# A norm factored out per token, a gather in halves, another load order, and attention by pairs of heads

## The reference

```
mod = silu(c) @ ada_w + ada_b                          # sh1, sc1, g1, sh2, sc2, g2
h = rmsnorm(x, norm_mix_g) * (1 + sc1) + sh1
x = x + g1 * conformer_conv(h)     # 1024 -> 2x1024, gate, 31 taps, layernorm, silu, 1024 -> 1024
h = rmsnorm(x, norm_ffn_g) * (1 + sc2) + sh2
x = x + g2 * hier_moe(h)           # 4 groups x 8 experts, the best 2 of one group, 1024 -> 512 -> 1024
x = rmsnorm(x, final_g)
x = layer_norm(ALPHA * x + mla(x)) # 16 heads, 64 + 32 wide for scores, 64 for values, causal, gated
x = layer_norm(ALPHA * x + moba(x))# 16 heads of 64, causal at this length, gated
```

## Time and profile before

| | |
|---|---|
| runs | 1060.81, 1059.29, 1056.29 us; median 1059.29 |
| profiled execution | 1058.31 us, span 1056.5 us, mean granted clock 0.974 |
| busy | PE 956.9 us (91%), DVE 280.9 (27%), ACT 201.9 (19%), POOL 186.5 (18%) |
| DMA | 285.94 MB, mean 271 GB/s |
| longest waits of PE | 21.7 us in 14 waits for expert up weights, 14.8 for the constants at the start |

### The profile page before, as it was taken

One profiled execution on the slowest core, in us unless ns is written; L12 is line 12 of the kernel. 1 busy time (PEld: TensorE's weight loads), 2 busy tenths in 40 slices (PEclk: granted clock), 3 DMA queues, 4 the chain that ended last, 5 costly groups with the idle time before them and its releaser, 6 DMA issues. The chain is left out here.

```text
span 1056.5 us, 13629 instructions
## 1 busy us (share of the span) xinstructions
PE 956.9 (91%) x5360; PEld 565.5 (54%) x5360; DVE 280.9 (27%) x741; ACT 201.9 (19%) x465; POOL 186.5 (18%) x310
## 2 busy tenths in 40 slices
PE   4799898989998988889888899699999889999996
PEld 3688686434443443334333343387667458487642
DVE  0499523411111000110001100313343336051223
ACT  1355323110000000000000000211124311013440
POOL 0067300021111111111111110001012101024213
PEclk9899899899999999999999999999999999999988
DMA  9993862449999999999999999912001943302001
GB/s 382 426 427 136 355 228 112 160 177 430 428 428 427 429 429 427 429 429 427 429 429 429 428 428 426 389 45 102 24 2 41 426 181 112 127 1 81 1 1 40
DMA packets 21935, 285.94 MB, mean 271 GB/s; under 512 B 2434, under 2 KB 3202, under 8 KB 4354
## 3 DMA queue, kind: packets, MB, share of 16 engines
q1 hardware_dynamic: 20880, 283.65, 64.8%
q10 hardware_dynamic: 1010, 1.67, 0.4%
HBM read 284.26 MB, written 1.05 MB: 270 GB/s over the span
## 5 line engine op out<-in xcount | busy, mean ns | idle before, releaser
L1031 PE MATMUL bank<-arena 128*64 128x512 f32 x1024 | 226.4, 594 | 34.5 <-DMA arena<-in_w_expert_up 21.7
L855 PE MATMUL bank<-arena 128*128 128x256 f32 (+1 forms) x912 | 202.8, 384 | 4.6 <-DVE arena L1593 3.0
L855 PEld LDWEIGHTS bank<-arena 128*128 128x128 f32 (+1 forms) x912 | 174.2, 192 | 32.1 <-issue 6.6
L1031 PEld LDWEIGHTS bank<-arena 128*64 128x64 f32 x1024 | 82.3, 137 | 177.2 <-issue 177.2
L1048 PE MATMUL bank<-arena 128*64 128x512 f32 x512 | 116.9, 598 | 0.8 <-ACT arena L717 0.8
L1561 DVE TENSOR_TENSOR arena<-bank,arena 64x512 f32<-64x512 f32 x32 | 21.9, 683 | 312.1 <-ACT arena L713 312.1
L717 ACT ACTIVATE arena<-bank 128x512 f32<-128x512 f32 x32 | 19.1, 597 | 381.9 <-PE bank L1040 381.9
L1048 PEld LDWEIGHTS bank<-arena 128*64 128x64 f32 x512 | 34.2, 136 | 65.8 <-issue 65.8
L515 POOL COPY der<-arena 128x4 f32 (+1 forms) x32 | 6.0, 187 | 347.3 <-PE bank L1040 323.9
L1058 PE MATMUL bank<-arena 64*128 64x256 f32 x512 | 65.7, 386 | 0.8 <-DVE arena L1564 0.8
L1392 DVE SCALAR_TENSOR_TENSOR bank<-arena,par,bank 128x256 f32<-128x256 f32 x152 | 61.9, 484 | 0.6
(11 more groups left out here) (217 smaller groups left out, 887.2 us busy)
## 6 DMA issues: line engine op xcount, KB each, us to landing
arena<-in_w_expert_gate SPq DMA_DIRECT2D x32, 2048.0 KB, 25.0
arena<-in_w_expert_up SPq DMA_DIRECT2D x32, 2048.0 KB, 29.4
arena<-in_w_expert_down SPq DMA_DIRECT2D x32, 2048.0 KB, 20.8
arena<-in_w_ada SPq DMA_DIRECT2D x11, 2048.0 KB, 24.1
arena<-in_w_glu SPq DMA_DIRECT2D x4, 2048.0 KB, 35.2
arena<-in_w_kv SPq DMA_DIRECT2D x4, 2048.0 KB, 19.9
arena<-in_w_in_b SPq DMA_DIRECT2D x4, 2048.0 KB, 8.0
arena<-in_w_uq SPq DMA_DIRECT2D x4, 1152.0 KB, 10.9
```

The lines of the kernel that those rows point to most:

```text
L855: mm = pe.matmul(bank[part:part + m, at:at + n], w[:, k, lo:lo + m], rhs[:, k0 + k, :], start=(k == 0), stop=(k == tiles - 1))
L1031: mm = pe.matmul(GU_BANK[half * WIN:(half + 1) * WIN, :], xw[b][:, k, :], w[:, k, :], start=(k == 0), stop=(k == KD - 1), skip_group_check ...
```

## The change

- x is loaded behind ada 0 alone, and the first total comes ahead of ada 1. The last channels of the convolution go in the order LAST, 5, 6, the mean total is split in three and interleaved, `ada_row(4)` moves into ACT's last products, `ada_row(8)` behind the silus, its columns behind `proj1(3)`.
- The second norm is never applied to all of x. The router's weights are scaled by a2 beforehand (wr2) and multiply the unnormed xT; the shift's share of the logits is made once (`shift_row`, `shift_all`). xT is turned to token rows between the projections; ACT squares these with a sum per token, and the root's reciprocal, one number per token, scales the logits and h2_tok. Gain and shift per channel are applied as the gathered banks are read.
- The gather runs in halves of 256 slots: the first ahead of the first expert, the second behind its gate and up matmuls. The banks are opened by `start` of the first combination.
- SP asks for gate and up of e+3, then down of e+2. In the last two experts `begin` stands ahead of `finish`.
- Attention goes by pairs of heads: scores of both, gate matmuls (8, 8, 6, 6, 4 in the first five pairs), transposes of the previous pair, parts of the output projection in steps 6 to 9, value matmuls of the pair before that, alternating between the two heads. ACT's silu of the gates moves from head 13 to pair 5, the rows of x from the last heads to the first two pairs.

```diff
-PE_ORDER = (0, 1, 2, 3, 4, 5, LAST, 6)
+PE_ORDER = (0, 1, 2, 3, 4, LAST, 5, 6)
+GATES_AT = 5
+GATE_PARTS = (8, 8, 6, 6, 4)
+OUT_PARTS = {6: (0, 1), 7: (1, 2), 8: (2, 4), 9: (4, 6)}
...
-                if chunks[i][0] == ("ada", 1):
+                if chunks[i][0] == ("ada", 0):
                     sp.dma_start(arena[:, R0:R], A["x_columns"]).then_inc(sem("x_in"), 16)
...
+            def refill(e, b, freed_gate_up, freed_down):
+
+                sp.wait_ge(gu_full, freed_gate_up)
+                load_matrix(e + BODY, b, 0)
+                load_matrix(e + BODY, b, 1)
+                if freed_down is not None:
+                    sp.wait_ge(y_full, freed_down)
+                    load_matrix(e + (BODY - 1), (b - 1) % BODY, 2)
...
             for j in range(KD):
-                products(j, 0, 4)
+                before = 4 if j < KD - 1 else 2
+                products(j, 0, before)
                 if j < KD - 1:
                     sigmoid(j + 1)
-                products(j, 4, 8)
+                else:
+                    ada_row(4, 0, 2)
+                products(j, before, 8)
                 if j >= 2 and j < KD - 1:
                     convolved(j - 2)
-            ada_row(4, 0, 2)
+            ada_row(6, 2, 2)
             convolved(5)
-            ada_row(6, 2, 2)
             convolved(6)
...
+            for g in range(3):
+                for t in range(NT):
+                    bank = tok_bank(act, t, g)
+                    act.activation(waste[:, t, TOK_GROUPS[g][0] * P:TOK_GROUPS[g][1] * P], bank, ACT.Square,
+                                   accum_out=squares[:, t, g:g + 1]).then_inc(sem("squares_ready"), 1)
+            act.wait_ge(sem("square_sums"), 1)
+            act.activation(std_tok, square_sums, ACT.Sqrt, bias=eps6, scale=1.0 / D).then_inc(sem("std_tok"), 1)
+            act.wait_ge(sem("rstd_tok"), 1)
+            for g in range(3):
+                lo, hi = TOK_GROUPS[g]
+                for t in range(NT):
+                    bank = tok_bank(act, t, g)
+                    act.activation(h2_tok[:, t, lo * P:hi * P], bank, ACT.Copy, scale=rstd_tok[:, t:t + 1]) \
+                        .then_inc(sem("tok_moved"), 1)
...
             convolve(4)
             ada(4, 2)
-            convolve(5)
+            convolve(LAST)
             ada_columns(4, 0, 2, 2 * P)
             ada(6, 2)
-            convolve(LAST)
+            add_to_mean(0, 4)
+            convolve(5)
             ada_columns(6, 2, 2, 2 * P)
+            add_to_mean(4, 6)
             convolve(6)
             add_sum(LAST)
-            total("mean1", y, KD, lambda k: moved(pe, ("conv", k)))
+            add_to_mean(6, KD)
             total("var1", sq, KD, lambda k: pe.wait_ge(sem("squared1"), k + 1))
             ada(8, 2)
...
+            for j in range(4):
+                proj1(j)
             ada_columns(8, 0, 2, 2 * P)
+            proj1(4)
+            token_major(0)
+            proj1(5)
             pe.wait_ge(sem("router_in"), 32)
-            bank = may_fill(pe, "logit_rows")
+            bank = may_fill(pe, "shift_row")
             for k in range(KD):
+                pe.matmul(bank[0:1, 0:CHOICES], mod[:, 24 + k:25 + k], wr[:, k, :], start=(k == 0), stop=False)
+            pe.matmul(bank[0:1, 0:CHOICES], ones[0:1, 0:1], brow[0:1, :], start=False, stop=True) \
+                .then_inc(full("shift_row"), 1)
+            proj1(6)
...
+            logits(0, 4)
+            proj1(7)
+            logits(4, 7)
+            token_major(1)
+            token_major(2)
+            logits(7, KD)
...
             for e in range(BODY):
                 begin(e, e, lambda s, back: EXPERT_BASE[s] + 16, first=e == 0)
+                if e == 0:
+                    gather(1)
...
                 e = LOOPS * BODY + b
+                begin(e, b, last_uses)
                 finish(e, b, last_uses)
-                begin(e, b, last_uses)
...
+                        for c in range(2):
+                            i = 2 * (n - 2) + c
+                            moved(pe, ("pt", layer, i))
+                            pe.matmul(bank[c * HD:(c + 1) * HD, 0:T], v[:, 0, i * HD:(i + 1) * HD],
+                                      prob_t[:, i % 4, 0:T], start=True, stop=False, skip_group_check=True)
...
+                for n in range(PAIRS + 3):
+                    if n < PAIRS:
+                        lowest(layer, 2 * n, scale)
+                    if 1 <= n <= PAIRS:
+                        b = (2 * n - 2) % 4
+                        dve.wait_ge(sem("exp_done"), 2 * (HEADS * layer + 2 * n))
+                        dve.reciprocal(srec[:, b:b + 2, :].rearrange("p b t -> p (b t)"),
+                                       ssum[:, b:b + 2, :].rearrange("p b t -> p (b t)")) \
+                            .then_inc(sem("sum_inverse"), 1)
+                    if n < PAIRS:
+                        lowest(layer, 2 * n + 1, scale)
+                    if n >= 3:
+                        merge(layer, n - 3)
```

## The result

| kernel | median of its runs, us | range, us | ratio to before, 95% interval | profiled execution, us | its span, us |
|---|---|---|---|---|---|
| before | 1057.8 | 1054.1 to 1060.8 | | 1058.31 | 1056.5 |
| after | 1022.3 | 1014.0 to 1024.4 | 0.965 (0.962 to 0.969) | 1023.14 | 1021.3 |

The account below looks back on a forecast made before the run. Bounds: engine waits before the first gate block, DMA in the expert stage, PE in the attentions. 21.15 + 3.1 + 4.4 + 11.6 = 40.25 off 1058.31 gives 1018.1, median 1019; range 1014 to 1028, with rivals 1010 to 1033.

Parts of the forecast that it names:

- Start: Kernel start: x issued one weight block sooner, total of squares behind one ada block, not two; gain 1.95 us, bounds 0 to 3.7.
- End of the convolution: Up to the mean total: reordering removes PE's 4.05 us idle but adds a 2.9 us wait; gain 1.15 us.
- proj1 starts earlier: Ahead of proj1: silu's table load no longer behind ada_row(8), mod columns moved behind proj1(3); gain 2.5 us.
- logits: From proj1 to the router's logits: total of squares, reciprocal, eight scalings and eight shifts removed; gain 4.35 us.
- first gate block: From logits to first gate block: shorter rank matmuls and only half the gather ahead; gain 11.2 us.
- Expert stage: Expert stage: up matrices land 4.9 us sooner, the stream loses 1.8 behind the first gate block; gain 3.1 us.
- T1: End of the first expert's gate and up block, when the first buffers come free; forecast to move by 21.15 us.
- the rival that ends slower: Expert stage: the stream runs dry at every down load, at 2 us an expert 1077 us; chance 0.02.
- First attention: First attention: paired value matmuls take 0.80 us a pair, not 1.60, with stalls in three pairs; gain 4.4 us.
- Second attention: Second attention and output: paired scores and value matmuls overlap, old idle and slow clock go; gain 11.6 us.
- The first rival: Attentions: heads' matmuls don't overlap or the chain is late for every pair; 12 us less gain, 1031; chance 0.15.
- the third (the clock stays up): Slow-clock allowances of 1.5, 3.3 and 1.8 us at the start come in as gain; 1012; chance 0.15.

Follow-up runs that it names:

- x_late: Changed kernel with x asked for behind the second weight block again, not the first; 1025.3 us, ratio 0.972.
- conv_old: Changed kernel with the end of the convolution back in the old order on PE and ACT; 1021.4 us, ratio 0.967.
- conv5_first: Changed kernel with PE's convolution of channel 5 back ahead of the last channel and ada(6); 1014.3 us, ratio 0.961.
- tail_old: Changed kernel with only the last loads of the expert stage back in the old order; 1022.7 us, ratio 0.969.
- one_by_one: Changed kernel with score and value matmuls of a pair's heads one head after the other, not interleaved; 1019.2 us, ratio 0.962.
- heads_apart: Changed kernel with the first head's value matmuls ahead of the step's transposes, the second's behind them; 1019.0 us, ratio 0.964.
- out_first: Changed kernel with a step's output matmuls ahead of its transposes in both attentions; 1011.3 us, ratio 0.957.
- three: Changed kernel with channel 5 ahead of the last, gathering in one piece before the experts, output matmuls ahead of transposes; 1002.3 us, ratio 0.949.
- four: The kernel three with each step's value matmuls ahead of its transposes too; 996.7 us, ratio 0.943.
- five: The kernel three with the constants asked for first and value matmuls ahead of the transposes; 998.5 us, ratio 0.947.
- consts_first: Changed kernel with the constants asked for ahead of the vectors on the scalar engine's DMA queue; 1024.1 us, ratio 0.970.

## Why the prediction was right, and where not

*Start (forecast 1.95, measured 5.14).* The mechanism held: the total of squares ends at 21.17, behind one ada block. What the sum lacked is that the constants land 2.6 us sooner (12.23 against 14.85); x_late shows that this is x's doing. 1.95 + 2.62 is 4.57; the rest is faster records, 0.3 us in the first row (3.40 us until the next, 3.71 before) and 0.3 in the last stretch ahead of the projections (5.18 and 5.50 us, granted clock 0.67 and 0.50). The bound of 3.7 was too low, since it took the start of PE's first row as given.

*End of the convolution (1.15; -2.56).* The forecast named the right chain: POOL's five additions behind PE's channel 5, ACT's products behind these, ada_row(6) behind both, PE idle 2.9 (measured 2.63). With its 1.5 for a slow stretch and less the 1.95 of the start the mean total was put at 124.15, and it ended at 124.21. That it fits is luck: the start had come 3.2 us sooner than assumed, and this was lost again, by 1.98 us of an idle time that I did not have and by 3.4 us of slow records where I had put 1.5 (the rows behind the two idle times, 2.40, 2.75, 1.92 and 2.27 us where full speed is 1.99, 1.46, 1.03 and 1.46). The error was less in a price than in taking the edit as a gain: by the traces of conv_old and conv5_first this order takes 3 us more than the old one and 8 more than the better one, and of the 8 about half lies at the idle time that no row explains.

*proj1 starts earlier (2.5; 2.53), logits (4.35; 5.38), first gate block (11.2; 10.49).* These held to within 1.1 us. The first choice of DVE is at 170.77, 38.17 us after proj1's start (forecast 39.2); of the shift's ten matmuls the rows show 0.68 + 0.22 + 0.41 = 1.3 us, where I had taken 2.2 between bounds of 0.6 and 4.3. The gate block follows the counts (178.26) by 14.35 us, where 13.9 was forecast, DVE's table (cast at 187.01) setting the second four channels of the gathering as described. Right for the named reasons; but the part of it that the halves bring is given back in the next step. The first gate block itself stood at 192.61 where 192.86 was forecast (214.01 less 21.15). That it is so close is luck, since 3.2 us too little at the start and 3.7 too much in the convolution cancel.

*Expert stage (3.1; 0.86).* Two terms, 4.9 and -1.8. tail_old shows the first (5.0 us of lateness, 6.6 with the clock). The second was mis-sized: from T1 the second gate block ended at 17.8, not 15.6 (the gathering 7.17 us with a wait of 1.95 behind it, and a block of 8.78 instead of 7.09 at a clock of 0.66), and the DMA idled 8.2 us against 4.0: -4.2. 4.9 - 4.2 = 0.7, measured 0.86. PE was behind until about expert 15, as forecast (busy 98.69 of the 100 us up to 399.7, 89.53 of the next 100), and the stream ran at 428 GB/s in both windows: the rival that ends slower did not come.

*First attention (4.4; 1.03).* The work came out: value matmuls of a pair 0.80, idle time before the transposes of steps 5, 6 and 7 of 1.81, 1.11 and 1.81 us (forecast 1.8 each) and 0.28 elsewhere, 5.0 in all. (These are the transposes of pairs 4 to 6, those of a pair stand one step behind its scores; the forecast names them by the step.) Missing in the sum was the clock. The old stretch had 1.00 throughout, the new one 0.92: behind the new idle time four output records take 3.62 us instead of 1.88, a pair's scores 3.15 instead of 1.74. one_by_one, the same work, was spared it (clock 1.00) although it idles as well (1.30 + 0.28 us in steps 5 and 6), and took 78.56 us, 5.9 less than before; the seven other traces took 81.57 to 84.23, 0.2 to 2.9 less. So the forecast's 4.4 came, and more, in the one trace of eight in which the clock stayed up; in the others (clock 0.92 to 0.96) much or nearly all of it is lost again. In the second attention I had put 3.3 us for that, here nothing; that is the step that failed.

*Second attention (11.6; 11.26).* The sum held, its terms only in part. The scores of a pair take 0.85, one slow stretch of 1.7 us came (forecast 3.3), the old idle time of 2.60 and its slow clock (0.94 over the old stretch, 0.98 over the new one, by the windows) are gone. The idle time is 8.0 us, where 6.8 was put: 1.0 of it stands in step 1 and 0.28 in step 4, and PE waiting for POOL in pairs 1 to 4 was one of my signs of being wrong. It came in small. And heads_apart shows that the value matmuls' share, priced at 0.80 a pair, is mostly exchanged against idle time. The rule that speaks against the pairs (the Trainium skill, "TensorEngine Tiling (Array Packing)", Performance Considerations) is borne out in that share, in kind: what TensorE saved was waited for, 13.0 us in 15 waits. The page speaks of the emptying of PSUM; the waits here are for the end of a chain that begins with it and ends in POOL's scaling in SBUF. It does not hold for the whole, since out_first gets 10 us by giving PE something to do in the meantime, with the chain untouched.

*Rivals.* Of the 5.0 us that are missing against 40.25, 3.4 lie in the first attention, 2.2 in the expert stage and 3.7 in the convolution, against 3.2 more at the start and 1.1 in a stage that the change does not touch (that stage took 104.1 to 109.8 us over the traces). The first rival was right in its mechanism for the value matmuls only; the third (the clock stays up) was the opposite of what came. The signs: the last combination started at 648.60 (forecast near 649), the scores of the second attention at 939.24 (near 934), and the DMA idled 8.2 us behind T1, not some 5. The chances that I gave add up to 0.99.

## What to carry to other kernels

In a stage that the DMA bounds, ask not when its first block starts but for how long the stream will run dry behind it: gathering in halves moved the first block by 6 us and the stage by nothing. Where a faster TensorE opens idle time, it can pay twice, by the wait and by the clock behind it; independent matmuls moved into the gap brought 10 us here where halving the value matmuls brought nothing that could be seen. And when an edit puts one engine's step behind another's block, follow the whole ring back to the first engine: five additions of 0.84 us, started 10 us late, cost 2.6 us of idle time and some 1.8 of slow records behind it.

## What the runs showed of the hardware

*A small transfer on another queue waits for the big ones.* The constants (128 KB, asked for at 1.23 us) landed at 14.64 and 14.85 with two ada blocks ahead of x, at 12.14 to 12.66 with one, and at 9.06 and 9.14 when they changed places with the vectors. The Trainium skill, "DMA: Bandwidth & Descriptors", section Queues, rings and completion order, says that a transfer's semaphore write comes only after every earlier write of the same DMA engine, across its queues. The landings here fit that; no run tells it from transfers that merely share the engines' rate.

*An idle time that belongs to a place in PE's instructions.* The 1.98 us before the mean total have no releaser in the trace. They are 1.94 to 2.28 us long over the traces with the changed order and end at 109.39 to 110.81, at 112.06 in x_late, which runs 2.3 later, always between the last record of ada(6) and the mean total. In three, four and five, where the eight records of channel 5 stand ahead, the idle time (0.68, 0.71 and 0.44 us) has moved forward into the ada block, behind 119 of its 128 records:

```profile
105.22 3.48 PE L900 MATMUL bank<-arena 128*32 128x128 f32 x119
109.39 0.52 PE L900 MATMUL bank<-arena 128*32 128x128 f32 x9 [0.68 <-issue]
```

So it goes with a place in the list of instructions rather than with a semaphore. But conv5_first, whose PE list is that of three up to here, has no such idle time. What goes along with it is a packet of the instruction queue (0.02 MB): it lies between 106 and 107 us in the traces of after, three and four, between 107 and 110 in those that idle later (x_late, consts_first and five among them), some 2 to 3 us ahead of the end of the idle time each time, while the weights keep the DMA at 98 to 100%; conv5_first has none between 103 and 112. Against it, conv_old has one between 110 and 111 and no such idle time. That PE waits for its own instructions there is my reading; no run shows it alone.
